# A two-block layer kernel on one Trainium2 core: GpSimd makes the low halves of 42 of the 172 weight units

## The reference, cut to what matters

```python
def hybrid_layer(x, ...):                       # first block, one layer
    proj = rmsnorm(x, g_mix) @ w_in
    y_fox = forgetting_attention(...)           # 8 heads of 64
    y_sc = sb * causal_dwconv(sc * sv, sc_conv_w)
    dn_qkv = silu(causal_dwconv(dn_qkv, dn_conv_w))
    y_dn = rmsnorm(gated_delta_rule(...), gain) * silu(z)      # 4 heads of 128
    merged = sum(einsum('bsnc,ncd->bsnd', ys, w_branch) * gates)
    x = x + merged @ w_o
    x = x + (silu(u_gate) * u_val) @ w_down     # u = causal_dwconv(rmsnorm(x) @ w_up)
    return x + sigmoid(rmsnorm(x) @ w_ple_gate) * (p @ w_ple)

def second_block(x, ...):                       # layer 0: attention and pooling; layer 1: linear attention
    for i in range(2):
        h = _rmsnorm(x, norm_mix[i])
        x = x + (attention_and_pool(h) if i == 0 else _gla_mixer(h, w_in, ...))
        x = x + square(relu(_rmsnorm(x) @ ffn_w1[i])) @ ffn_w2[i]
    return _rmsnorm(x, norm_final)
```

## Time and profile before

| | |
|---|---|
| median of 3 runs | 1252.39 us (1250.83 to 1253.11) |
| the profiled execution, its own time | 1251.72 us |
| its span from first to last instruction | 1250.0 us |
| TensorE busy | 1168.1 us, 93% of the span |
| VectorE busy | 780.1 us, 62% |
| ScalarE busy | 556.6 us, 45% |
| GpSimd busy | 41.5 us, 3% |
| low halves on VectorE (line 1109) | 172 of 2291 ns mean, 393.8 us |
| high halves on ScalarE (line 740) | 172 of 1911 ns mean, 327.8 us |

### The profile page before, as it was taken

One profiled execution on the slowest core, in us unless ns is written; L12 is line 12 of the kernel. 1 busy time (PEld: TensorE's weight loads), 2 busy tenths in 40 slices (PEclk: granted clock), 3 DMA queues, 4 the chain that ended last, 5 costly groups with the idle time before them and its releaser, 6 DMA issues. The chain is left out here.

```text
span 1250.0 us, 17910 instructions
## 1 busy us (share of the span) xinstructions
PE 1168.1 (93%) x7678; PEld 1047.7 (84%) x7678; DVE 780.1 (62%) x916; ACT 556.6 (45%) x635; POOL 41.5 (3%) x103
## 2 busy tenths in 40 slices
PE   7797989989989999999897999999989899999997
PEld 6586988889878999998786789999878867999996
DVE  4287855654455898887677464555567835655454
ACT  5373454522345444344555354344443534544433
POOL 8000000000000000000000300000000000000000
PEclk9899989989999999999999899999989999999999
DMA  7644847533334565554553355555543423556551
GB/s 246 156 108 85 139 119 131 120 88 68 102 122 134 190 203 181 190 180 157 168 182 126 110 170 184 187 188 183 169 136 102 134 68 102 193 181 199 179 192 51
DMA packets 128449, 185.10 MB, mean 148 GB/s; under 512 B 6868, under 2 KB 104161, under 8 KB 128370
## 3 DMA queue, kind: packets, MB, share of 16 engines
q1 hardware_dynamic: 123136, 182.46, 48.7%
q10 hardware_dynamic: 4690, 1.36, 0.5%
q0 software_dynamic: 544, 0.13, 0.0%
HBM read 182.89 MB, written 1.05 MB: 147 GB/s over the span
## 5 line engine op out<-in xcount | busy, mean ns | idle before, releaser
L740 ACT ACTIVATE whi<-raw 128x2048 fp32r<-128x2048 f32 x172 | 327.8, 1911 | 359.0 <-PE ps L1751 176.9
L1109 DVE TENSOR_TENSOR wlo<-raw,whi 128x2048 fp32r<-128x2048 f32 x172 | 393.8, 2291 | 75.0 <-ACT whi L740 72.1
L1749 PE MATMUL ps<-hhi,whi 128*128 128x256 f32 x1424 | 411.8, 289 | 16.6 <-ACT conv L827 7.5
L1750 PE MATMUL ps<-hlo,whi 128*128 128x256 f32 x1424 | 406.2, 285 | 0.0
L1751 PE MATMUL ps<-hhi,wlo 128*128 128x256 f32 x1424 | 406.0, 285 | 0.0
L1749 PEld LDWEIGHTS ps<-hhi,whi 128*128 128x128 f32 x1424 | 276.5, 194 | 26.0 <-issue 13.1
L1750 PEld LDWEIGHTS ps<-hlo,whi 128*128 128x128 f32 x1424 | 276.7, 194 | 1.9 <-issue 0.5
L1751 PEld LDWEIGHTS ps<-hhi,wlo 128*128 128x128 f32 x1424 | 276.3, 194 | 0.0
L1766 PE MATMUL ps<-whi,ahi 128*128 128x512 f32 x416 | 165.3, 397 | 6.8 <-issue 4.5
L1767 PE MATMUL ps<-wlo,ahi 128*128 128x512 f32 x416 | 164.0, 394 | 0.0
L1768 PE MATMUL ps<-whi,alo 128*128 128x512 f32 x416 | 163.7, 393 | 0.0
(11 more groups left out here) (374 smaller groups left out, 1261.1 us busy)
## 6 DMA issues: line engine op xcount, KB each, us to landing
raw<-in_ffn_w SPq DMA_DIRECT2D x64, 1024.0 KB, 5.3
raw<-in_w_in SPq DMA_DIRECT2D x32, 1024.0 KB, 10.7
raw<-in_w_up SPq DMA_DIRECT2D x22, 1024.0 KB, 5.1
raw<-in_gla_w_in SPq DMA_DIRECT2D x12, 1024.0 KB, 5.2
raw<-in_w_down SPq DMA_DIRECT2D x11, 1024.0 KB, 5.0
raw<-in_ab_w_in SPq DMA_DIRECT2D x8, 1024.0 KB, 5.7
raw<-in_w_branch SPq DMA_DIRECT2D x6, 1024.0 KB, 7.6
raw<-in_w_o SPq DMA_DIRECT2D x4, 1024.0 KB, 5.0
```

The source lines that it names most:

```text
L740: act.activation(whi[:, u % SPLIT, :], raw[:, u % RAW, :], ACT.Copy).then_inc(sem("hi_done"), 1)
L1109: dve.tensor_tensor(wlo[:, u % SPLIT, :], raw[:, u % RAW, :], whi[:, u % SPLIT, :].bitcast(F32), ALU.subtract).then_inc(sem("lo_done"), 1)
L1749: pe.matmul(out, wh, hi[:, k0 + k, :], start=k == 0, stop=False)
L1750: pe.matmul(out, wh, lo[:, k0 + k, :], start=False, stop=False)
```

## The change

GpSimd gets the low halves of 42 units: 6 to 37 (the front behind the first six) and 126 to 135 (the linear attention behind its first two). They are collected in `by_pool` from the steps that use a unit's product; the first two units behind a normalisation are left out. Each is made as four subtractions of 128 x 512 in place of one of 128 x 2048. GpSimd walks `order` too and makes the low half of u + 2 at the step `mm(u, 0)`, a step part earlier than VectorE did. The units of VectorE still count `lo_done`; those of GpSimd count a new semaphore `pool_low`; TensorE and SP wait for the one that `low_ready` names. The window sums of the pooling stay in their place in the order and are wrapped into a function. Six semaphores that were each raised once by TensorE (`gmix_turned`, `colp_turned`, `dn_ss`, `dn_gc`, `p_turned`, `pool_mmed`) become one counter, `pe_single`.

```diff
+    by_pool = set()
+    for s in order:
+        if s[0] in ("dn", "sc", "z", "gate", "merge", "gla_qk", "gla_g"):
+            by_pool.add(s[-1])
+        elif s[0] == "gla_v":
+            by_pool.update(range(s[1] - 3, s[1] + 1))
+    by_pool -= set(fresh) | {u + 1 for u in fresh}
+    low_ready = []
+    for u in range(NU):
+        low_ready.append(("pool_low" if u in by_pool else "lo_done",
+                          1 + sum((v in by_pool) == (u in by_pool) for v in range(u))))
...
                 if u >= RAW:
-                    sp.wait_ge(sem("lo_done"), u - RAW + 1)
+                    sp.wait_ge(sem(low_ready[u - RAW][0]), low_ready[u - RAW][1])
...
+            def split_low(u):
+                pool.wait_ge(sem("hi_done"), u + 1)
+                for at in range(0, UNIT, UNIT // 4):
+                    s = slice(at, at + UNIT // 4)
+                    ins = pool.tensor_tensor(wlo[:, u % SPLIT, s], raw[:, u % RAW, s],
+                                             whi[:, u % SPLIT, s].bitcast(F32), ALU.subtract)
+                ins.then_inc(sem("pool_low"), 1)
...
+            last_u = [s for s in order if s[0] == "pool_u"][-1]
+            for s in order:
+                if s[0] == "mm" and s[2] == 0 and s[1] + LEAD in by_pool:
+                    split_low(s[1] + LEAD)
+                if s == last_u:
+                    window_means()
...
             def split_low(u):
+                if u in by_pool:
+                    return
                 dve.wait_ge(sem("hi_done"), u + 1)
...
                 if part == 0:
-                    pe.wait_ge(sem("lo_done"), u + 1)
+                    pe.wait_ge(sem(low_ready[u][0]), low_ready[u][1])
```

More of the change, by code:

```diff
@@ L631, in build @@
         made = {}
+        single = [s[0] for s in order if s[0] in ("norm_first", "params", "dn_square", "dn_cum", "ple_p", "pool_mm")]
+        single = {name: 1 + at for at, name in enumerate(single)}
         loaded = {"gmix": 16, "ple": 32, "pool": 64, "gla": 96, "nfin": 112}
@@ new lines, in window_means, with chained @@
+            def window_means():
+                for ready in [took(s[2]) for s in order if s[0] == "pool_u"]:
+                    pool.wait_ge(*ready)
+                E_ = W0 + T
+                src, sums = pu, (p1, p2, p3, p4)
+                def chained(ins):
+                    n[0] += 1
+                    ins.then_inc(sem("constants"), 1)
+                    pool.wait_ge(sem("constants"), n[0])
+                chained(pool.memset(pu[:, :, 0:W0], 0.0))
+                for l, dst in enumerate(sums):
+                    s = 1 << l
+                    at = 2 * s - 1
+                    chained(pool.tensor_tensor(dst[:, l:4, at:E_], src[:, l:4, at:E_], src[:, l:4, at - s:E_ - s], ALU.add))
+                    src = dst
+                for g, w in enumerate(POOLS):
+                    pool.tensor_tensor(pfix[:, g, :], sums[g][:, g, W0:W0 + 16], inv[:, g, :], ALU.mult)
+                    chained(pool.tensor_scalar(pr[:, g, 16:T], sums[g][:, g, W0 + 16:E_], 1.0 / w, None, ALU.mult))
+                pool.tensor_tensor(pr[:, :, 16:T], pr[:, :, 16:T], pu[:, :, W0 + 16:E_], ALU.subtract)
+                pool.tensor_tensor(pr[:, :, 0:16], pfix, pu[:, :, W0:W0 + 16], ALU.subtract).then_inc(sem("pool_r"), 1)
@@ L942, in ple_p @@
             def ple_p():
-                act.wait_ge(sem("p_turned"), 1)
+                act.wait_ge(sem("pe_single"), single["ple_p"])
                 act.activation(ahi[:, 4:6, :], tiles(ps[:, 6, :]), ACT.Copy).then_inc(sem("ple_hi"), 1)
@@ L1362, in dn_cum @@
             def dn_cum():
-                dve.wait_ge(sem("dn_gc"), 1)
+                dve.wait_ge(sem("pe_single"), single["dn_cum"])
                 pg = ps[:, 6, 0:TT * 2 * DH].rearrange("p (t a h) -> p t a h", t=TT, a=2)
@@ L1558, in pool_mm @@
             def pool_mm():
-                dve.wait_ge(sem("pool_mmed"), 1)
+                dve.wait_ge(sem("pe_single"), single["pool_mm"])
                 for g in range(4):
@@ L1808, in params @@
                     ins = pe.transpose(ps[:, 7, b * P:(b + 1) * P], rows[:, b, :], ident[:, :])
-                ins.then_inc(sem("colp_turned"), 1)
+                ins.then_inc(sem("pe_single"), 1)
             def small():
@@ L1912, in dn_cum @@
                         ins = pe.matmul(ps[:, 6, at:at + DH], m[:, :], gg[:, t, :], start=True, stop=True)
-                ins.then_inc(sem("dn_gc"), 1)
+                ins.then_inc(sem("pe_single"), 1)
             def dn_tok(t):
@@ L2023, in ple_p @@
                         ins = pe.transpose(ps[:, 6, at:at + P], ptok[:, t, k * P:(k + 1) * P], ident[:, :])
-                ins.then_inc(sem("p_turned"), 1)
+                ins.then_inc(sem("pe_single"), 1)
             def pool_mm():
@@ L2031, in pool_mm @@
                                     start=True, stop=True)
-                ins.then_inc(sem("pool_mmed"), 1)
+                ins.then_inc(sem("pe_single"), 1)
             def ab_turn(b):
```

10 lines of the change are left out of this document (5 added, 5 removed).

## The result

The changed kernel took 1269.57 us (median of 4 runs, 1268.54 to 1269.98) beside 1251.61 of before (4 runs): 1.43% slower, ratio 1.0143 [1.0126, 1.0161]. The forecast was 1257 with a range to 1268: the direction was right, the size was not, and the time lies outside the range. The profiled execution has a span of 1267.6 us, 17.6 more than before.

The account below looks back on a forecast made before the run. TensorE was taken to wait mainly for VectorE's chain, in which low halves stand. Front +8, delta rule -4 and linear attention +1 gave +5: profiled 1250.0 becomes 1256.7, forecast 1257 us, 8-in-10 range 1233 to 1268.

Parts of the forecast that it names:

- The mechanism and its price: GpSimd pieces and VectorE operations with two SBUF inputs exclude each other; each piece that meets one costs VectorE 1.05 us.
- free case: Rival, whole kernel: pieces cost VectorE next to nothing; -19 us, 1233 us; chance 0.13.
- GpSimd's time: GpSimd's low halves: 1.1 us for 512 columns, 4.7 us a unit with gaps, against 2.29 on VectorE.
- GpSimd as the bound: Rival, linear attention levels: pieces also wait for VectorE, GpSimd falls behind, TensorE waits; +9 beyond the sum, 1266 us; chance 0.12.
- Unit 8: Early front: GpSimd has the low half ready later than VectorE did, so TensorE starts late; +2.6 us, bounds +1.4 and +4.
- Twelve pieces in a row: Front, first two tiles' taps: units 8 to 10 made at once delay VectorE; +2.4 us beyond unit 8's.
- Three turns of the front: Front up to 125 us: four pieces a unit cost 4.2 us and replace 2.29; +1.2 us net in each turn.
- Behind 125 us TensorE has no wait on this chain: Later front: what is lost before stays, and what VectorE saves later buys nothing; no further term.
- Delta rule: Units after the front: waits behind low halves shrink by 2.3, 1.6 and 1.0, pieces met elsewhere add 0.9; sum -4 us.
- Linear attention: Units 126 to 135: -2.6 us at one wait, +3.5 over five levels; sum +1 us.
- The wait at its start: Linear attention: a 3.48 us TensorE wait for a bank had a low half right ahead; its removal gives -2.6 us.
- The levels: Linear attention: pieces lengthen VectorE's work, 8.1 us a level instead of 7.4; +0.7 in each of five, +3.5 us.

Follow-up runs that it names:

- e12_places: Changed kernel with GpSimd's subtractions replaced by constant fills, plus 15.5 us of VectorE reductions at fifteen places in the linear attention; 1245.34 us, 0.9955 of the kernel before.
- e4: Changed kernel with GpSimd making the low halves of units 26 to 37 and 126 to 128 alone, in four pieces; 1248.66 us, 0.9976 of the kernel before.

## Why the prediction was right and wrong

- *The mechanism and its price* (1.05 us for each piece that meets a two-input operation): right. Alone, the engines show 1.00 us; in the layer 0.85 to 1.15 for 49 of the 69 instructions that were longer by 0.15 us or more. The kernel without the reading took 1234 us where the prediction's free case said 1233, but that match is in part luck: its fills are done in 2.7 us a unit and hold some scalings up, neither of which the free case has. The rule of the Trainium skill (SBUF — State Buffer, Who interferes with whom) holds for both directions here: 682 to 1679 ns for VectorE's addition, and 1262 to 1706 ns for GpSimd's piece beside it.
- *GpSimd's time*: 1.1 us a piece and 4.7 a unit were forecast, 1.26 and 5.0 measured where nothing met them. GpSimd as the bound did not happen.
- *Unit 8*, +2.6: right (+2.7, start at 79.0, all of it a wait). *Twelve pieces in a row*, +2.4: +2.2 by unit 10, but by luck, for TensorE does not wait there; these 2.2 us are matmuls at a clock of 0.88 for 1.00.
- *Three turns of the front*, +3.6: measured +6.9 from unit 10 to 13, 4.4 of it waits (with what the twelve pieces cost in waits) and 2.5 longer matmuls. *"Behind 125 us TensorE has no wait on this chain"*: wrong. The waits for L1377 (the low half of the attention's output) and L1418 (the decays) grew by 1.0 and 3.2 us, the latter by two-input instructions, the former behind a copy that waited 0.86 us for its raw buffer, which the sum had priced at nothing; 1.4 came back at unit 14, and units 13 to 26 lost 2.0 net. The front was +13.9 for +8.6.
- *Delta rule*, -4: measured -4.1, but only 2.2 of it are waits; 1.9 are shorter matmuls, which the sum did not have, so the size is partly luck.
- *Linear attention*, +1: measured +7.2. The wait at its start fell as forecast (3.48 to 0.7; -2.6 in that window). The levels, forecast +0.7 in each of five, took 8.3 us more together, 5.0 of waits and 3.3 of longer matmuls, and the stretch behind them 3.2 more, all of it longer matmuls.
- *The step that failed*, under all of these: the sum counted waits and gave no time to TensorE's clock. The waits alone were +9.1 for the forecast +5 (front +8.1, for 8.6; delta rule -2.2; linear attention +2.2, for 1; before unit 6, 0.9; the rest 0.1). With them alone the forecast would have come out at 1261. The other 8.5 us are matmuls that ran longer: +5.8 in the front at 0.88 to 0.94, -1.9 in the delta rule, +5.0 in the linear attention, where a stretch that ran at 1.00 fell to 0.83. `e12_places` gave the same 0.83 by VectorE's longer work, without GpSimd's reading. But e4 lost 4.7 us to the clock with no wait added, so it is not shown how much clock a given wait costs, and for the front no run took waits and clock apart. A second, smaller part is that VectorE's losses were spread over a turn or level by their mean, while what counts is whether they stand ahead of what TensorE waits for: 14.2 us spread evenly cost 6.3, 15.5 us at the places 11.3.
- *The range* ended at 1268 because the only case above the forecast was GpSimd as the bound. Its own width, 7 us either way, had no term for the clock either.

## What to carry to other kernels

Moving elementwise work to GpSimd relieves VectorE little where VectorE works with two SBUF inputs: each piece of 512 columns that meets such an instruction cost it about 1 us of the piece's 1.26. Instructions with an input in PSUM lost nothing, so put such work beside those, and try the piece size: one, four, eight and sixteen gave 3.9, 1.4, 0.5 and 2.7% more time here, and eight in chosen units 0.75% less. Changed waits of TensorE can change its clock too: here 9.1 us of new waits came with 8.5 us of longer matmuls, and in one run 4.7 us of longer matmuls came with no new wait. Give the range a term for that.

## What was not expected of the hardware

- Fills on GpSimd, which only write, lengthened VectorE's scaling of one SBUF input from 351 to 1083 ns in the mean, and no two-input instruction. Four of twelve scalings were held for 1.5 to 2.8 us, each until all fills of a unit were through.
- GpSimd's one-input copy of 512 columns took 1.49 us, longer than its subtraction of two (1.26).
- With eight or sixteen short pieces in a row single VectorE instructions were kept out for 6 to 12 us. It could not be brought about with subtractions beside VectorE on the two engines alone, and its cause is open. The scalings beside the fills may be a case of the same; that is not shown.
- The granted clock fell from 1.00 to 0.84 in one stretch of e4 where GpSimd was idle, VectorE's work as before and TensorE's waits no longer. What set it off is open.
